# Seven products of 256 tokens in place of eight: Strassen's method in the gate/up layers of two feed-forward blocks

## What is computed

```python
def rmsnorm(x, g):
    x32 = x.astype(jnp.float32)
    y = x32 * lax.rsqrt(jnp.mean(x32 * x32, axis=-1, keepdims=True) + EPS)
    return (y * g.astype(jnp.float32)).astype(x.dtype)

def swiglu(h, w_gate, w_up, w_down):
    return (jax.nn.silu(h @ w_gate) * (h @ w_up)) @ w_down

for i in range(DEPTH):            # DEPTH = 2
    ...
    h = rmsnorm(x, norm_ffn[i])
    x = x + swiglu(h, ffn_w_gate[i], ffn_w_up[i], ffn_w_down[i])
```

## Time and profile before

| | |
|---|---|
| median of 3 runs | 1773.09 us (1773.04 to 1773.48) |
| profiled execution | span 1771.1 us from first to last instruction, 21509 instructions; the runs' times hold about 2 us around such a span |
| PE busy | 1743.0 us, 98% |
| weight loads (PEld) | 1395.6 us, 79% |
| DVE, ACT, POOL busy | 992.9, 713.7, 273.0 us (56%, 40%, 15%) |
| DMA | 163.35 MB, mean 92 GB/s |
| mean granted TensorE clock | 0.996 of full speed |

### The profile page before, as it was taken

The page is one execution under the profiler, slowest core; times in us unless marked ns, Lnnn a source line. Parts: engine busy times, 40 slices in busy tenths (PEclk is TensorE's granted clock), DMA queues, the critical chain, the costliest instruction groups (busy, mean ns, idle before and its releaser), DMA issues.

```text
span 1771.1 us, 21509 instructions
## 1 busy us (share of the span) xinstructions
PE 1743.0 (98%) x8282; PEld 1395.6 (79%) x8282; DVE 992.9 (56%) x1260; ACT 713.7 (40%) x1058; POOL 273.0 (15%) x207
## 2 busy tenths in 40 slices
PE   9999999999999999999999999999999999999997
PEld 6885888888888777888888888766677778888887
DVE  6997554424444555654424434559735687437753
ACT  6876332212232343432212233465664444314432
POOL 2993200000001000200000004572201200000002
PEclk9999999999999999999999999999999999999999
DMA  5210432222232311222222232523212223322221
GB/s 186 96 51 31 125 112 104 101 79 91 105 115 72 127 60 42 93 112 102 104 75 93 101 124 83 150 75 111 67 48 72 71 71 107 119 72 95 104 98 48
DMA packets 28918, 163.35 MB, mean 92 GB/s; under 512 B 4607, under 2 KB 7819, under 8 KB 12460
## 3 DMA queue, kind: packets, MB, share of 16 engines
q1 hardware_dynamic: 25664, 156.28, 25.4%
q10 hardware_dynamic: 3180, 6.07, 1.1%
HBM read 154.98 MB, written 4.47 MB: 90 GB/s over the span
## 4 chain that ended last, share of the span: by engine, by line
PE 83%; DVE 7%; POOL 6%; ACT 2%; issue 1%; DMA 0%; POOLq 0%; ACTq 0%; DVEq 0%
PE PS L646 26%; PE PS L648 25%; PE PS L647 25%; POOL CV L1939 4%; DVE W_lo L2071 1%; ACT W_hi L1294 1%; POOL ISC L2003 1%; PE PS L1113 1%; PE PS L1092 1%; PE PS L1104 0%; DVE WK L2494 0%; PE PS L943 0%; PE PS L977 0%; DVE TOP L2492 0%; DVE H_lo L2051 0%
## 5 line engine op out<-in xcount | busy, mean ns | idle before, releaser
L646 PE MATMUL PS<-H_hi,W_hi 128*128 128x512 f32 x1600 | 638.5, 399 | 7.3 <-DVE W_lo L2071 2.0
L648 PE MATMUL PS<-H_hi,W_lo 128*128 128x512 f32 x1600 | 624.1, 390 | 0.0
L647 PE MATMUL PS<-H_lo,W_hi 128*128 128x512 f32 x1600 | 623.9, 390 | 0.0
L1294 ACT ACTIVATE W_hi<-W_raw 128x2048 fp32r<-128x2048 f32 (+2 forms) x130 | 262.7, 2021 | 673.1 <-PE PS L648 673.1
L646 PEld LDWEIGHTS PS<-H_hi,W_hi 128*128 128x128 f32 x1600 | 300.8, 188 | 91.5 <-issue 23.0
L2071 DVE TENSOR_TENSOR W_lo<-W_raw,W_hi 128x2048 fp32r<-128x2048 f32 (+2 forms) x130 | 334.1, 2570 | 60.4 <-ACT W_hi L1294 60.0
L648 PEld LDWEIGHTS PS<-H_hi,W_lo 128*128 128x128 f32 x1600 | 300.6, 188 | 63.7
L647 PEld LDWEIGHTS PS<-H_lo,W_hi 128*128 128x128 f32 x1600 | 301.1, 188 | 58.5 <-issue 1.0
L1891 POOL TENSOR_TENSOR SSUM<-SSUM,SQ 128x512 f32<-128x512 f32 x43 | 63.3, 1472 | 1330.6 <-ACT SQ L1337 1328.9
L646 PE MATMUL PS<-HID_hi,W_hi 128*128 128x512 f32 x618 | 240.9, 390 | 1.5 <-DVE HID_lo L2190 1.4
L647 PE MATMUL PS<-HID_lo,W_hi 128*128 128x512 f32 x618 | 240.4, 389 | 0.0
(11 more groups left out here) (344 smaller groups left out, 1571.1 us busy)
## 6 DMA issues: line engine op xcount, KB each, us to landing
W_raw<-in_inp SPq DMA_DIRECT2D x13, 1024.0 KB, 4.9
W_raw<-in_pw SPq DMA_DIRECT2D x11, 1024.0 KB, 4.8
W_raw<-in_gu0a SPq DMA_DIRECT2D x11, 1024.0 KB, 4.9
W_raw<-in_gu0b SPq DMA_DIRECT2D x11, 1024.0 KB, 4.8
W_raw<-in_gu1a SPq DMA_DIRECT2D x11, 1024.0 KB, 4.8
W_raw<-in_gu1b SPq DMA_DIRECT2D x11, 1024.0 KB, 4.9
W_raw<-in_gu2a SPq DMA_DIRECT2D x11, 1024.0 KB, 4.8
W_raw<-in_gu2b SPq DMA_DIRECT2D x11, 1024.0 KB, 4.9
```

The costliest lines, as they stand in the source:

```text
L646: nc.tensor.matmul(dst[:], wh, x_hi[:, k, :], start=(k == first), stop=False)
L647: nc.tensor.matmul(dst[:], wh, x_lo[:, k, :], start=False, stop=False)
L648: return nc.tensor.matmul(dst[:], wl, x_hi[:, k, :], start=False, stop=(k == last))
L1294: nc.scalar.activation(W_hi[b][:, 0:n], W_raw[b][:, 0:n], ACT.Copy).then_inc(w_hi, 1)
```

## The change

The weight block of a unit is cut in 2 × 2 (even or odd feature tiles, by gate or up columns) and the activations in 2 × 2 (even or odd feature tiles, by first or second 256 tokens). Strassen's scheme (in Winograd's form) computes the four result quarters from seven block products, not eight, of combined operands.

- PE: `strassen_unit` runs 7 parts × 4 tiles × 3 = 84 matmuls of 256 tokens, where `unit` ran 48 of 512. Accumulators are shared between parts, so copies have to be taken within a unit: PE waits at parts 3, 4 and 5 until ACT has copied an earlier sum out (`part_taken`), and at parts 4, 5 and 6 for the weight combinations in SLOT_hi/SLOT_lo (`slot_lo`).
- POOL: makes four weight combinations per unit out of W_raw (`sums12`: two of W_sum, `sums43`: SUM4 and SUM3) and multiplies the up half by R (`up_half`).
- DVE: splits the weights in five pieces (W_lo in two of 1024, three slots of 512), adds the PSUM quarters to the copies (four additions of 256), multiplies the gate half by R.
- ACT: three PSUM copies of 256, and five weight pieces in place of one.
- pw2 and wo: `pair_steps` in place of `add_steps`. ACT scales X to Z, DVE makes four differences of 256 tokens per pair of tiles (EZ and one in place), both split the pair and the three differences (E_hi, E_lo).
- Units 0 and 1 of gu0a and gu1a have an order of their own, since R is not known yet.
- Buffers: W_hi and W_lo hold 8 tiles, the down layers' other 3 are in tail buffers; the split of a down unit is two instructions, not one. Five constant matrices that nothing used are dropped from cmat.

```diff
+            def strassen_part(L, b, i, k, first, last):
+                dst = quarters(L, b)[(0, 1, 2, 0, 1, 0, 3)[i]]
+                if i < 4:
+                    c = BLOCK * (0, 2, 1, 3)[i] + P * k
+                    wh, wl = W_hi[b][:, c:c + P], W_lo[b][:, c:c + P]
+                else:
+                    wh, wl = SLOT_hi[i - 4][:, P * k:P * k + P], SLOT_lo[i - 4][:, P * k:P * k + P]
...
+                nc.tensor.matmul(dst, wh, xh, start=start, stop=False, skip_group_check=True)
+                nc.tensor.matmul(dst, wh, xl, start=False, stop=False, skip_group_check=True)
+                return nc.tensor.matmul(dst, wl, xh, start=False, stop=last, skip_group_check=True)
...
+                for i in range(PARTS):
+                    if i == 3:
+                        pe.wait_ge(part_taken, j.v(4, TAKEN0 + 4 * L.parts + 1))
+                    if i == 4:
+                        pe.wait_ge(part_taken, j.v(4, TAKEN0 + 4 * L.parts + 2))
+                        pe.wait_ge(slot_lo, j.v(3, SLOT0 + 3 * L.parts + 1))
+                    if i == 5:
+                        pe.wait_ge(part_taken, j.v(4, TAKEN0 + 4 * L.parts + 3))
+                        pe.wait_ge(slot_lo, j.v(3, SLOT0 + 3 * L.parts + 2))
+                    if i == 6:
+                        pe.wait_ge(slot_lo, j.v(3, SLOT0 + 3 * L.parts + 3))
...
+            def sums12(L, j):
...
+                nc.gpsimd.tensor_tensor(one, raw_block(b, 0, 1), raw_block(b, 1, 1), ALU.add).then_inc(sums_made, 1)
+                pool.wait_ge(sums_made, j.v(4, SUMS0 + 4 * L.parts + 1))
+                nc.gpsimd.tensor_tensor(two, one, raw_block(b, 0, 0), ALU.subtract).then_inc(sums_made, 1)
+            def sums43(L, j):
...
+                nc.gpsimd.tensor_tensor(blocked4(SUM4[L.base % 2][:]), raw_block(b, 1, 0), two, ALU.subtract).then_inc(sums_made, 1)
...
+                nc.gpsimd.tensor_tensor(blocked4(SUM3[:]), raw_block(b, 0, 0), raw_block(b, 0, 1), ALU.subtract).then_inc(sums_made, 1)
...
+                def up_half(j, own):
+                    if own:
+                        pool.wait_ge(r_made, norm + 1)
+                    pool.wait_ge(acc_free, j.v(1, L.base + 1))
+                    y = T_hid if own else T_u
+                    nc.gpsimd.tensor_tensor(y[:], y[:], R[:], ALU.mult).then_inc(up_scaled, 1)
...
+                for m in (2 * j, 2 * j + 1):
+                    act.wait_ge(x_ready, X_BASE[norm] + m + 1)
+                    nc.scalar.activation(Z[:, m, :], X[:, m, :], ACT.Copy, scale=vec(gain, m)).then_inc(z_made, 1)
...
-                    nc.vector.tensor_tensor(T_g[:], PS[2 * b][:], R[:], ALU.mult).then_inc(gate_in, 1)
...
-                    nc.vector.tensor_tensor(T_u[:], PS[2 * b + 1][:], R[:], ALU.mult).then_inc(acc_free, 1)
```

More of the change, by code:

```diff
@@ L196, in build @@
     order = [layers[x[0]] for x in LAYERS]
[L197 removed]
+    of_unit = [l for l in order for _ in range(l.n)]
     vec_at, n_vec = {}, 0
@@ L648, in product, with products @@
                 return nc.tensor.matmul(dst[:], wl, x_hi[:, k, :], start=False, stop=(k == last))
[L650 to L654, removed]
+            def products(b, L, half, x_hi, x_lo, between=None):
+                for k in range(L.kt):
+                    last = product(b, L, half, k, x_hi, x_lo)
+                    if between is not None and k % 2 and k < L.kt - 1:
                         between()
@@ L825, in _ @@
                 for half in range(2):
-                    last = product(0, L.kt, half, k, H_hi, H_lo)
+                    last = product(0, L, half, k, H_hi, H_lo)
                     if k == L.kt - 1:
@@ L834, in _ @@
                     for k in range(L.kt):
-                        last = product(j % 2, L.kt, half, k, H_hi, H_lo)
+                        last = product(j % 2, L, half, k, H_hi, H_lo)
                         if k == L.kt - 1:
@@ new lines, in strassen, with step @@
+            def strassen(name, norm=None):
+                L = layers[name]
+                def step(j):
+                    first = j.i is None and j.c == 0 and norm is not None
+                    second = j.i is None and j.c == 1
+                    strassen_unit(L, j, norm if first else None, norm if second else None)
+                    if first:
+                        rms_sum(norm)
+                steps(pe, L.n, step, first=2, last=1)
+            def feed_forward(l, norm):
+                if f"gu{l}a" in STRASSEN:
+                    strassen(f"gu{l}a", norm)
+                    linear(f"dn{l}a", HID_hi, HID_lo, ready=after(hid_lo_made, gu_base[f"gu{l}a"]))
+                    strassen(f"gu{l}b")
+                    linear(f"dn{l}b", HID_hi, HID_lo, ready=after(hid_lo_made, gu_base[f"gu{l}b"]))
+                    return
@@ L1262, in _ @@
                 for half in range(2):
-                    last = product(L.base % 2, L.kt, half, k, H_hi, H_lo, first=4, last=3)
+                    last = product(L.base % 2, L, half, k, H_hi, H_lo, first=4, last=3)
                     if k == 3:
@@ L1963, in _, with squares_and_sums @@
+            def squares_and_sums(norm, L):
+                for m in range(DT):
+                    if m == 5:
+                        sums12(L, At(0))
+                        sums43(L, At(0))
+                    add_square(norm, At(m))
+            squares_and_sums(FFN0, layers["gu0a"])
+            strassen_steps("gu0a", FFN0)
+            sums12(layers["gu0b"], At(0))
+            sums43(layers["gu0b"], At(0))
+            strassen_steps("gu0b")
             add_squares(MIX1)
```

538 lines of the change are left out of this document (443 added, 95 removed).

## The result

The kernel before ran in 1773.07 us (median of 4 runs, 1772.90 to 1773.48), the changed one in 1879.33 us (median of 4, 1878.28 to 1883.51): 6.0% slower, a ratio of 1.0605 with an interval of 1.059 to 1.062. The forecast was 1867 us, 1800 to 1900.

A forecast was written before the change was run, and what follows sets the result against it. PE's matmuls were taken to bound the kernel before, the read port shared by DVE and POOL the changed one. Span 1771.1 + 84.4 (units) + 10 (norm) = 1865.5, and 2 around it: 1867 us, range 1800 to 1900.

The forecast's parts named there:

- PE's pitch of 119.9 ns: Gate/up units on PE: 256-token matmuls start 119.9 ns apart, so 84 of them take 10.07 us.
- the gain of 35.6 us: PE in 44 gate/up units: 0.81 us less each, at most 35.6 us, coming to nothing inside the +84.4.
- The order of turns: Settled gate/up unit: DVE and POOL take the port first come first served, D12, P1, D1 through P5, D7; round 13.1 us.
- The units: Four gate/up layers: 140.8 us each against 119.7, settled units at 13.1 us, +84.4 us in all.
- Around the norm: pw2, wo and the first gate/up units: extra differences, lag and the reciprocal, +10 us in all, between 3 and 16.
- the likeliest case: Whole kernel: the forecast itself, 1835 to 1880 us, chance 0.59.
- I take 5 us per block: Around the norm: the assumed loss for each of two blocks, 10 us in all, between 3 and 16.
- 2 us of lag: wo's units: 8.2 us long for about 10 of DVE's and POOL's turns, so 2 us per unit can reach gu1a.
- The port costs nothing: Rival, gate/up units: DVE's and POOL's instructions fall side by side, unit 10.07 us, whole 1747 us, chance 0.11.
- Rests less than in my layout: Rival, settled units: port shared more finely or without rest, 11.6 us, whole 1809 us, or 1777 with 10.8; chance 0.13.
- The narrow hold of 1.09 us: POOL's port hold per instruction counting only what grows with size, 1.09 us; port work 10.8 us a unit.
- The clock falls: Rival, settled units: parts 4 and 5 at 1.2 GHz after PE's rest, round 13.65 us, +20, 1887 us, chance 0.13.

The follow-up runs named there:

- e8: Kernel before, gu0b and gu1b in calls of 256 tokens, gu1b with 84 matmuls a unit, no POOL work: 1770.75 us.
- e2: Changed kernel with POOL's five operations per gate/up unit each cut to 8 columns plus fills that read nothing: 1773.69 us.
- e3: Changed kernel with only POOL's up half times R replaced by 8 columns and fills, weight sums kept: 1842.31 us.
- e5: e4 with the reciprocal of the two blocks' norms on 8 columns and a copy of the rest: 1867.79 us.
- e9: e6 with unit 0's SLOT_lo behind the last pair and PE running ahead with parts 0 to 2 alone: 1889.77 us.
- e13: e11 with POOL's first two sums for unit 1 of gu0a and gu1a ahead of the squares of tiles 6 and 7: 1872.02 us.
- e4: Changed kernel with POOL's weight sums for unit 0 of gu0a and gu1a one square earlier, whole computation: 1871.82 us.
- e11: e4 with DVE's T_g+=PS addition of 256 moved between T_hid and HID_lo: 1874.27 us.
- e14: e11 with ACT's W_hi<-W_sum moved from behind T_u<-PS to ahead of HID_hi: 1873.68 us.
- e6: e4 with T_u*R moved from POOL to DVE ahead of T_hid, whole computation: 1887.16 us.

## Why the prediction was right

**Right in sign and mechanism.** PE's pitch of 119.9 ns, and with it the gain of 35.6 us that is swallowed, is confirmed by e8. The port as the cause of the longer unit is confirmed by e2; e3 agrees with it. The order of turns is the layout's, and so is what closes the round: a row of port turns from D12 to D7, then silu, a copy and D9 to D11. PE waits where it was forecast, 2.30 us in the unit shown against 3.0. The four PSUM additions stayed at 0.41 to 0.42.

**Two terms were mis-sized, and most of the errors cancelled.** The units: +84.4 forecast, +66.2 measured. Around the norm: +10 forecast, +38.0 measured, outside the 3 to 16. Together they put the forecast 9.8 us too low, and 1.0 us is lost ahead of pw2: 1771.1 + 66.2 + 38.0 + 1.0 gives the span of 1876.3. That the time came within 1% of 1867, and 0.7 us inside the 1835 to 1880 of the likeliest case, is in part luck.

The settled round was laid out at 13.1 and is 12.65. Of the 0.46 in the unit shown, 0.16 lie in the row of port turns (10.21 us from D12's start at 294.10 to D7's end at 304.31, forecast 10.37) and 0.3 in the rest, where I had put more time between the engines than they take.

The step that failed is "I take 5 us per block": e2 shows 31 of the 38 us with POOL's reads gone, so most of it is dependences and queues, not the port. PE waits 6.19 us ahead of gu0a and 8.9 ahead of gu1a for SLOT_lo, where I had 0 to 2 and "2 us of lag". I had counted the last pair's chain, but not that unit 0's split stands ahead of it on DVE and waits 3.97 us for POOL's sums. Then W_lo of units 1 and 2 wait for POOL again, 4.85 and 2.12 us, and the reciprocal adds to it; e5 took 2.7 us of PE's waiting out of each block. A cost that I had not counted at all is the clock in these first units: it was at 0.50 for PE's first matmuls of gu0a, again in part 5 of unit 0 and at the start of unit 2, each time from within or just behind a rest of PE (the row is unit 2's start, behind a rest of 5.1 us):

```profile
250.80:254.90 4.10, 4.10 (x21) 4.10 (x21) 4.07 (x4) 2.36 (x5) 2.23 (x2) 0.50 0.00 0
```

Matmuls start 0.21 us apart there in place of 0.12. By the length of these stretches PE loses some 4.5 us in each of gu0a and gu1a, an estimate, and the waits behind take in part of it. e2 has such stretches too, so they are in its 31. Of the rest no single cause was isolated; e9 and e13 show that a reordering mostly moves it.

**The rivals.** "The port costs nothing" fell with e2. "Rests less than in my layout", 11.6, was not reached: 2.43 us of each round lie behind D7, with only D8 and D10 on the port, so it rests some 1.2 us. The narrow hold of 1.09 us for POOL in that rival had no row behind it; e2 (last section) puts the part of a POOL addition that does not grow with size at 0.20 us, which leaves the same 1.09. "The clock falls" was right in what happened and wrong in what it costs in a settled unit. Windows of the changed kernel over two neighbouring rounds, then over 312 to 316 us (the clock is the ninth entry):

```profile
293.77:306.41 12.64, 10.34 (x86) 10.14 (x85) 11.00 (x13) 5.91 (x12) 9.29 (x5) 1.00 0.24 83
306.41:319.04 12.63, 10.30 (x74) 10.11 (x73) 10.84 (x14) 5.71 (x11) 9.22 (x5) 0.86 0.25 83
...
312.00:316.00 4.00, 3.48 (x18) 3.49 (x19) 3.33 (x5) 2.25 (x5) 3.73 (x3) 0.62 0.00 0
```

After PE's rest ahead of part 4 the clock was granted at 1.2 GHz for part of the second round, 0.62 on average over those 4 us, and the round is 12.63, as long as the first: PE's next wait is 0.8 us in place of 2.3. With some 6 us of a round at 1.2 GHz, as in e4 and e5, the round is 14.5 to 14.8.

**Open.** The 2.43 us behind D7 were not attacked. POOL stands idle 3.14 us there, and an order that puts one of its turns into that time, or D7 ahead of P5, wasn't tried; e3, in which D7 did come ahead of P5, is no test of it, as it had a turn fewer. A variant in which DVE reads R from PSUM, so that its scalings leave the port, wasn't tried either.

## What to carry to other kernels

Before work is taken off PE, price what the sums and scalings cost the engines around it: here 0.81 us a unit on PE was bought with five POOL instructions that each held the port for about 1.1 us. Lay such a unit out in turns, not in busy shares; DVE was busy 68% of the span and still late. And price the first units after a stage in which the queues are ordered otherwise by themselves, waits behind waits, since the steady round says nothing of them. Then look for the closed chain of turns and waits that makes the round, before moving anything: an edit off that chain gives nothing, as e11 and e14 did. To shorten the row of turns, the turns must become fewer.

## What the runs showed of the hardware

- Moving a scaling from the slower holder of the port (1.13 us) to the faster (0.61) made the kernel slower: 1887.16 against 1871.82 us.
- A POOL addition of 8 columns takes 0.20 us when nothing holds the port (e2, below), one of 512 takes 1.29: nearly all of its length grows with the size. The 0.58 us in e2's timeline above stand beside DVE's SLOT_lo. Fills of 72 columns take 0.15 us each and start 0.09 us apart.
- 3.4 us of PE at 1.2 GHz in a round cost nothing in the middle of a layer of the changed kernel (12.63 us), since PE was not what the round waited for. Some 6 us cost 1.7 to 2.1 (14.51 in e4's gu1b, 14.76 in e5's gu0a); in e6, whose turns lie otherwise, 0.3 (13.4 for 13.1).
- The same layer with the same code differed by 1.75 us between two kernels that differ only elsewhere (gu1b, 136.22 after and 137.97 in e4), by the stretch at 1.2 GHz in one of its rounds.

```profile
L2247 POOL TENSOR_TENSOR SUM<-W_raw x44: 197/200/530, 210.9 to 1026.3; 128x8 f32<-128x8 f32 x44
```
